# Feed-forward output of a two-layer trunk: one 512-column matmul for the high and low left tiles, two adds for its two halves

## What is computed

```python
D_MODEL, SEQ, DEPTH, D_FF = 1024, 512, 2, 2816

def swiglu(h, w_in, w_out):
    gate, up = jnp.split(h @ w_in, 2, axis=-1)
    return (jax.nn.silu(gate) * up) @ w_out

for layer in range(DEPTH):
    x = x + 0.5 * swiglu(rmsnorm(x, norm_ffn1[layer]), w_ffn1_in[layer], w_ffn1_out[layer])
    x = x + mixer(rmsnorm(x, norm_mix[layer]))          # retention, then sparse attention
    x = x + 0.5 * swiglu(rmsnorm(x, norm_ffn2[layer]), w_ffn2_in[layer], w_ffn2_out[layer])
return rmsnorm(x, final_norm)
```

## Time and profile before

| | |
|---|---|
| median of 3 runs | 1930.58 us |
| lowest, highest | 1929.31, 1930.98 us |
| the profiled execution, its own time | 1932.33 us |
| span of its profile, first to last instruction | 1929.5 us |
| TensorE (PE) busy | 1908.6 us |
| VectorE (DVE) busy | 1590.9 us |
| ScalarE (ACT) busy | 992.3 us |
| GpSimd (POOL) busy | 189.5 us |
| mean granted TensorE clock | 0.998 of 2.4 GHz |

### The profile page before, as it was taken

The page is one execution under the profiler, slowest core; times in us unless marked ns, Lnnn a source line. Parts: engine busy times, 40 slices in busy tenths (PEclk is TensorE's granted clock), DMA queues, the critical chain, the costliest instruction groups (busy, mean ns, idle before and its releaser), DMA issues.

```text
span 1929.5 us, 27001 instructions
## 1 busy us (share of the span) xinstructions
PE 1908.6 (99%) x10772; PEld 1666.0 (86%) x10772; DVE 1590.9 (82%) x1903; ACT 992.3 (51%) x1296; POOL 189.5 (10%) x164
## 2 busy tenths in 40 slices
PE   9999999999999999999999999999999999999998
PEld 7888899888888888888899888889997898888998
...
GB/s 207 207 205 235 214 207 181 118 137 44 137 44 137 95 123 91 205 207 193 254 166 180 177 231 182 207 258 150 177 84 88 1 45 256 202 191 200 264 185 84
DMA packets 100524, 316.63 MB, mean 164 GB/s; under 512 B 5936, under 2 KB 14128, under 8 KB 97328
## 3 DMA queue, kind: packets, MB, share of 16 engines
...
...
## 4 chain that ended last, share of the span: by engine, by line
PE 91%; DVE 4%; ACT 2%; issue 2%; DMA 1%; POOL 1%; SPq 0%; DVEq 0%; POOLq 0%; ACTq 0%
PE bank L2819 14%; PE bank L2821 14%; PE bank L2820 14%; PE bank L2987 7%; PE bank L2989 7%; PE bank L2988 7%; PE bank L2811 4%; PE bank L2813 4%; PE bank L2812 4%; PE bank L3043 3%; PE bank L3045 3%; PE bank L3044 3%; PE bank L2920 2%; PE bank L3054 1%; DVE part_lo L1809 1%
## 5 line engine op out<-in xcount | busy, mean ns | idle before, releaser
L1206 ACT ACTIVATE part_hi<-quad_w 128x1024 fp32r<-128x1024 f32 x280 | 293.1, 1064 | 280.5 <-PE bank L2821 196.4
L1809 DVE TENSOR_TENSOR part_lo<-quad_w,part_hi 128x1024 fp32r<-128x1024 f32 x280 | 329.9, 1217 | 25.5 <-ACT part_hi L1206 25.3
L2819 PE MATMUL bank<-part_hi,s_hi 128*128 128x512 f32 x640 | 252.4, 394 | 0.6 <-DVE part_lo L1809 0.6
L2821 PE MATMUL bank<-part_hi,s_lo 128*128 128x512 f32 x640 | 249.4, 390 | 0.0
L2820 PE MATMUL bank<-part_lo,s_hi 128*128 128x512 f32 x640 | 249.1, 389 | 0.0
L2819 PE MATMUL bank<-part_hi,xn_hi 128*128 128x512 f32 x608 | 238.1, 392 | 2.4 <-DVE part_lo L1809 2.3
L2821 PE MATMUL bank<-part_hi,xn_lo 128*128 128x512 f32 x608 | 237.3, 390 | 0.0
L2820 PE MATMUL bank<-part_lo,xn_hi 128*128 128x512 f32 x608 | 237.1, 390 | 0.0
L1971 DVE TENSOR_TENSOR quad_w<-quad_w,quad_w 128x1024 f32<-128x1024 f32 x160 | 188.5, 1216 | 1.1
L1233 ACT ACTIVATE part_hi<-quad_w 128x1024 fp32r<-128x1024 f32 x84 | 87.0, 1058 | 148.7 <-PE bank L2813 105.9
L2821 PEld LDWEIGHTS bank<-part_hi,s_lo 128*128 128x128 f32 x640 | 120.1, 188 | 25.3
...
...
## 6 DMA issues: line engine op xcount, KB each, us to landing
...
```

The costliest lines, as they stand in the source:

```text
L1206: nc.scalar.activation(in_four(part_hi[part_slot(h)]), source, copy).then_inc(part_hi_made, 1)
L1809: nc.vector.tensor_tensor(in_four(part_lo[part_slot(h)]), source, in_four(part_hi[part_slot(h)]).bitcast(FP32), ALU.subtract)\
L2819: mm(to, hi, in_four(part_hi[slot])[:, :, part], start=start, stop=False, skip_group_check=joins)
L2821: return mm(to, lo, in_four(part_hi[slot])[:, :, part], start=False, stop=stop, skip_group_check=joins)
```

## The change

High and low left tiles are moved by one matmul. Where the weight tile `out_hi` met `left_hi` (L2987) and then the low tile (L2988) in two matmuls of 256 columns into the same 256 sums, it now meets both in one matmul of 512 columns. The moving operand is an access pattern over a common tensor, `left_arena`, with two runs of 256 columns; the two results go into the two halves of a whole bank. The third matmul (`out_lo` with `left_hi`) is added to the lower half as before. The two halves are added only when the bank is read: `add_out` issues two adds, one for each half, the second waiting for the first (`link`).

A tile `dt` now takes a bank of its own. Y has banks 0 to 3, and V and Z share the upper four (`upper_banks`), so that S1T1 must wait for the adds P2 that read x12w21 from the same banks, a wait that was not there before. Some more waits are changed for the same reason: steps of x11w11 and x12w21 wait for the instructions that last read their banks, the last group's turned tiles go to four banks instead of two, and a sublayer behind a feed-forward block waits until the first half of its last add is made. P1 a moves four places back in VectorE's queue. Step 3 of the chain Z in the last block keeps the old form (`one_width`).

```diff
@@ -250,9 +249,7 @@
-    left_hi = [at(f"left_hi{n}", a, HALF_TILES * HALF_SEQ, FP32R)
-               for n, a in enumerate((room, room + 2 * left_size))]
-    left_lo = [at(f"left_lo{n}", a, HALF_TILES * HALF_SEQ, FP32R) for n, a in enumerate(left_lo_at)]
+    left_hi_at = (room, room + 2 * left_size)
...
@@ -265,6 +262,17 @@
+    arena_at = left_lo_at[1]
+    arena_width = (left_hi_at[1] + left_size - arena_at) // 4
+    left_arena = at("left_arena", arena_at, arena_width, FP32R)
+
+    def of_arena(offset, width):
+
+        return left_arena[:, (offset - arena_at) // 4:(offset - arena_at) // 4 + width]
+
+    left_hi = [of_arena(a, HALF_TILES * HALF_SEQ) for a in left_hi_at]
+    left_lo = [of_arena(a, HALF_TILES * HALF_SEQ) for a in left_lo_at]
+    gated_lo = of_arena(gated_at, FF_TILES * SEQ)
...
@@ -374,7 +382,8 @@
     t_sums = nc.dram_tensor("t_sums", (SUBLAYERS.count("ffn") * len(T_SUMS) * OUT_TILES, P, OUT_UNIT), FP32).ap()
-    bank = [ctx.enter_context(nc.psum_tensor(f"bank{n}", [P, SEQ], FP32)) for n in range(8)]
+    banks = ctx.enter_context(nc.psum_tensor("banks", [P, 8 * SEQ], FP32))
+    bank = [banks[:, SEQ * n:SEQ * (n + 1)] for n in range(8)]
     def sem(name):
         return ctx.enter_context(nc.semaphore(name))
@@ -620,13 +629,29 @@
         half, tokens = {"S3T3": (0, 0), "x22T4": (1, 1), "S4w22": (1, 0)}[name]
         return gated_tiles(gated_lo, half, tokens, *LEFT_BATCHES[p][j])
-    def left_low_tile(p, k):
+    def left_low_at(p, k):
         name = OUT_PRODUCTS[p]
         if name in ("x11w11", "x12w21", "S1T1", "S2T2"):
-            return cols(left_lo[p % 2], k, HALF_SEQ)
+            return left_lo_at[p % 2] + 4 * HALF_SEQ * k
         half, tokens = {"S3T3": (0, 0), "x22T4": (1, 1), "S4w22": (1, 0)}[name]
-        return cols(gated_lo, HALF_TILES * half + k)[:, HALF_SEQ * tokens:HALF_SEQ * (tokens + 1)]
+        return gated_at + chunk * (HALF_TILES * half + k) + 4 * HALF_SEQ * tokens
+
+    def left_parts(p, k):
+
+
+        both = sorted([left_hi_at[p % 2] + 4 * HALF_SEQ * k, left_low_at(p, k)])
+        return bass.AP(left_arena, (both[0] - arena_at) // 4,
+                       [[arena_width, P], [(both[1] - both[0]) // 4, 2], [1, HALF_SEQ]])
+
+    def left_low_tile(p, k):
+
+        return bass.AP(left_arena, (left_low_at(p, k) - arena_at) // 4, [[arena_width, P], [1, HALF_SEQ]])
+
+    def one_width(s, chain, dt):
+
+
+        return chain == "Z" and s == len(SUBLAYERS) - 1 and dt == OUT_TILES - 1
     def chain_of(p):
@@ -637,14 +662,17 @@
         return [(0, 2), (2, 3), (3, 4)] if chain == "Z" and s == len(SUBLAYERS) - 1 else [(0, 2), (2, 4)]
+    def upper_banks(s):
+
+        return (4, 5, 6, 7) if s + 1 < len(SUBLAYERS) and SUBLAYERS[s + 1] == "ret" else (6, 7, 4, 5)
+
     def out_bank(s, chain, dt):
-        if chain == "Z" and s == len(SUBLAYERS) - 1 and dt == OUT_TILES - 1:
-            return 6, 0
-        first = {"Y": 0, "V": 2, "Z": 4}[chain]
-        if s + 1 < len(SUBLAYERS) and SUBLAYERS[s + 1] == "ret":
-            first = {"Y": 0, "V": 4, "Z": 2}[chain]
-        return first + dt // 2, dt % 2
+        return dt if chain == "Y" else upper_banks(s)[dt]
+
+    def turned_bank(s, g, half, n):
+
+        return 6 + n if g < GROUPS - 1 else upper_banks(s)[2 * half + n]
     def x_adds(s):
@@ -1322,7 +1350,8 @@
                         to = gated_raw[:, :].rearrange("p (n t) -> p n t", n=FF_TILES)
                         first = GROUP_TILES * g + 2 * n
                         nc.scalar.activation(to[:, first:first + 2, HALF_SEQ * half:HALF_SEQ * (half + 1)],
-                                             bank[6 + n][:, :].rearrange("p (n t) -> p n t", n=2), copy)\
+                                             bank[turned_bank(s, g, half, n)].rearrange("p (n t) -> p n t", n=2),
+                                             copy)\
                             .then_inc(gated_stored, 1)
                 def store_rest():
@@ -2102,14 +2131,17 @@
                     (a, b), chain = piece, chain_of(p)
-                    n, first = out_bank(s, chain, a)
+                    n = out_bank(s, chain, a)
                     columns, tokens = {"x11": (0, 0), "x12": (1, 0), "x21": (0, 1), "x22": (1, 1)}[name]
                     x = x_res[:, :].rearrange("p (k t) -> p k t", k=CHUNKS)
                     to = x[:, OUT_TILES * columns + a:OUT_TILES * columns + b,
                            HALF_SEQ * tokens:HALF_SEQ * (tokens + 1)]
-                    made = bank[n][:, :].rearrange("p (d t) -> p d t", d=2)[:, first:first + b - a]
+                    made = banks[:, SEQ * n:SEQ * (n + b - a)].rearrange("p (d i t) -> p d i t", d=b - a, i=2)
                     dve.wait_ge(unit_done, u0 + OUT_TILES * p + b)
-                    done = nc.vector.scalar_tensor_tensor(to, made, factor, to, ALU.mult, ALU.add)
+                    done = nc.vector.scalar_tensor_tensor(to, made[:, :, 0], factor, to, ALU.mult, ALU.add)
+                    if not one_width(s, chain, a):
+                        link(done)
+                        done = nc.vector.scalar_tensor_tensor(to, made[:, :, 1], factor, to, ALU.mult, ALU.add)
                     if part is None:
                         done.then_inc(x_updated, b - a)
                     else:
@@ -2200,11 +2232,11 @@
                 gated_2(GROUPS - 1)
                 out_low(3)
                 two = pieces(s, "Y")
-                add_out("x11", 0, two[0], "P1", 0.5)
                 out_low(4)
                 out_low(5)
                 left_low(1, 0)
                 left_low(1, 1)
+                add_out("x11", 0, two[0], "P1", 0.5)
                 sum_left("S1")
                 out_low(6)
                 add_out("x11", 0, two[1], "P1", 0.5)
@@ -2857,6 +2889,8 @@
             u0 = FIRST_UNIT[s]
             g0, m = groups_before(s), sums_before(s)
             norm = ("norm", s)
+            if s > 0 and SUBLAYERS[s - 1] == "ffn":
+                pe.wait_ge(x_updated, CHUNKS * (s - 1) + OUT_TILES + 2)
             if kind == "ffn":
                 f = ffn_of(s)
                 parts0 = PARTS * f
@@ -2913,11 +2947,13 @@
                     from_, made = ((v, gated1_made), (p5, gated2_made))[half]
                     pe.wait_ge(made, 2 * (GROUPS * f + g + 1))
+                    if g == GROUPS - 1:
+                        pe.wait_ge(up1_made, 2 * (g0 + GROUPS))
                     for n in range(2):
                         pe.wait_ge(gated_stored, TURNED * f + 4 * g + 2 * half + n + 1)
                         for m in range(2):
                             for t in range(2):
-                                done = nc.tensor.transpose(tile(bank[6 + n], 2 * m + t),
+                                done = nc.tensor.transpose(tile(bank[turned_bank(s, g, half, n)], 2 * m + t),
                                                            tile(from_[t], 2 * n + m), identity[:, :])
                         done.then_inc(gated_turned, 1)
@@ -2955,14 +2991,19 @@
                     p, dt = i // OUT_TILES, i % OUT_TILES
                     name, chain = OUT_PRODUCTS[p], chain_of(p)
-                    n, first = out_bank(s, chain, dt)
                     piece = next(q for q in pieces(s, chain) if q[0] <= dt < q[1])
                     ab = "ab"[dt // 2]
-                    if name == "x11w11":
+                    if name == "x11w11" and dt == 0:
                         pe.wait_ge(gate1_made, 2 * (g0 + GROUPS))
+                    elif name == "x11w11" and dt == 2:
+                        pe.wait_ge(gate2_summed, 2 * (g0 + GROUPS))
                     elif name == "x12w21" and dt == 0:
                         pe.wait_ge(up1_made, 2 * (g0 + GROUPS))
-                        pe.wait_ge(gate2_summed, 2 * (g0 + GROUPS))
+                        pe.wait_ge(gated_stored, TURNED * (f + 1) - 2)
+                    elif name == "x12w21" and dt == 2:
+                        pe.wait_ge(gated_stored, TURNED * (f + 1))
+                    elif name == "S1T1":
+                        pe.wait_ge(x_added, x_added_count(s, f"x11 P2 {ab}"))
                     elif name == "S2T2":
                         pe.wait_ge(x_added, x_added_count(s, f"x11 P1 {ab}"))
                     elif name == "S3T3":
@@ -2972,20 +3013,24 @@
                     elif name == "S4w22":
                         pe.wait_ge(x_added, x_added_count(s, f"x22 P5 {piece[0]}"))
                     pe.wait_ge(w_lo_made, u0 + i + 1)
-                    to = cols(bank[n], first, HALF_SEQ)
-                    opens = name in ("x11w11", "x12w21", "S1T1") and dt == piece[0]
-                    closes = dt == piece[1] - 1
-                    joins = name in ("S2T2", "S3T3", "x22T4", "S4w22")
+                    both = bank[out_bank(s, chain, dt)]
+                    to = cols(both, 0, HALF_SEQ)
+                    opens = name in ("x11w11", "x12w21", "S1T1")
+                    joins = not opens
                     _, hi, lo = out_bufs(i)
```

(12 more changed lines are left out.)

1 line of the change is left out of this document (removed).

## The result

The changed kernel takes 1953.16 us (median of 5 runs, 1951.58 to 1956.14), the kernel before 1930.98 us (5 runs, 1929.31 to 1933.57). The ratio is 1.0117, with a 95% interval of 1.0105 to 1.0129: slower by 22 us, inside the range forecast (1936 to 1956) and 5.3 us above the forecast of 1947.9. The profiled executions differ by 21.9 us of span.

The account below looks back on a forecast made before the run. TensorE, busy for 99% of the span, was taken as the bound. Waits net of TensorE's savings gave +10.9 us and the clock +6.4, so 1930.6 + 17.3 = 1947.9 us, range 1936 to 1956.

Parts of the forecast that it names:

- TensorE's work: Output part, 28 units (0 to 27) per block: 1210 matmul pairs each 0.0133 us shorter, 16.1 us in all at most.
- 0.146 less per unit: Each output unit on TensorE shrinks from 3.96 to 3.816 us.
- units 9 to 15: Output units after unit 8, not held by VectorE: forecast to save 4.0 us over the four blocks.
- VectorE's work: Each output add becomes two linked adds: a pair costs 1.31 us, 0.71 more than one add.
- 40 adds: The forecast's count of VectorE's output adds, said to be on no path by themselves.
- The new wait at unit 8: S1T1 waits for add P2 a to free its bank: 4.56 us later in block 0, 2.50 in others, 12.06 in all.
- Unit 18: It waits for add P6 b, 0.71 us lost per block; with units 16, 17 and 19, +1.7 us in all.
- The block's ends: Last adds delay the next work by 2.13, 1.42 and about 0.5 us in blocks 0, 2 and 3: sum 4.05.
- The clock: TensorE's clock falls after the idle at unit 8, 1.6 us lost per block: 6.4 us, bounds 0 and 12.8.
- It falls more often or longer: Rival, chance 0.12: clock falls more often or longer, at block ends too; +10.9 + 9 to 16 us, 1950 to 1957.
- the case that the forecast gave 0.50: Clock lost at unit 8 as forecast, once per block: +17.3 us, 1947.9 us.
- faster: Rival, chance 0.07: unit 8 doesn't wait in effect, 1914.5 us; decided by a pair costing no more than one add, 1926.1.

Follow-up runs that it names:

- Experiments 8: Against experiment 6's kernel: adds P2 b and x21 b also moved up in VectorE's queue; 1920.55 us, ratio 0.9945 to the kernel before.
- 9: Against experiment 8's kernel: the 512-column matmul written as two of 256 columns; 1931.45 us, ratio 1.0004 to the kernel before.
- experiment 2: Against the kernel before: each add to the stream made twice with half the factor, the second linked behind the first; 1940.07 us, ratio 1.0044.
- experiments 1: Against the changed kernel: the two adds of P2 a moved ahead of the sum S2 in VectorE's queue; 1940.47 us, ratio 1.0051 to the kernel before.
- 6: Against the changed kernel: adds P2 a, P6 a and P6 b moved up in VectorE's queue; 1929.49 us, ratio 0.9994 to the kernel before.
- experiment 10: Against the kernel before: only the add x21 b moved ahead of out_low(26); 1930.08 us, ratio 0.9999.
- Experiment 4: Against the changed kernel: 14 more 512-column matmuls ahead of unit 8's wait for P2 a; 1944.96 us, ratio 1.0086 to the kernel before.
- experiment 3: Against the changed kernel: the second add of each pair left out; 1930.24 us, ratio 0.9996 to the kernel before.

## Why the prediction came out right

**TensorE's work.** Units of 3.82 us came where forecast, but only half the time. Two stretches of block 0 in the changed kernel, the first short, the second long (answers to the earlier trace rows):

```profile
249.18 0.39 PE L3032 MATMUL banks<-left_arena,out_hi_C 128*128 128x512 f32 x1
249.41 0.27 PE L3034 MATMUL banks<-left_arena,out_lo_C 128*128 128x256 f32 x1
249.52 0.39 PE L3032 MATMUL banks<-left_arena,out_hi_C 128*128 128x512 f32 x1
```

```profile
318.72 0.40 PE L3032 MATMUL banks<-left_arena,out_hi_E 128*128 128x512 f32 x1
318.96 0.28 PE L3034 MATMUL banks<-left_arena,out_lo_E 128*128 128x256 f32 x1
319.08 0.40 PE L3032 MATMUL banks<-left_arena,out_hi_E 128*128 128x512 f32 x1
```

0.34 to 0.35 us for the three products of a tile, and 0.35 to 0.36. Of the undisturbed units 4 to 26 of all blocks 38 took 3.81 to 3.82 us and 37 took 3.88 to 3.89. The term "0.146 less per unit" was too large for half of them: units 9 to 15 saved 2.65 us, not 4.0. Experiments 8 and 9 give the term as a whole: 10.9 us of the 16.1. The figure of the Trainium skill that the forecast set against its own price (TensorE: Matmul & The Clock Gate, "Back-to-back issue gap": 2.5 ns on top of the columns for an isolated matmul, an estimate of 3 us in all) is too small for this stream with a weight load for each matmul: the two experiments give 9 ns for each of 1210.

**VectorE's work.** A pair takes 0.71 + 0.61 us (268.61, 269.32, 269.93), as worked out, with the second add starting 0.03 after the end of the first. The pairs on x12 and x21 have 0.79 between their starts, 0.08 more than forecast. The forecast's 40 adds (ten per block in the text ahead of it) are a miscount: the kernel before makes 58, 14 in each block and 16 in the last, and 56 of them are pairs now, which is VectorE's 38.6 us of added busy time (1629.5 for 1590.9). No sum used the 40.

**The new wait at unit 8**: right in mechanism. That the sum came out so close, 11.65 for 12.06, was luck: two errors of opposite sign nearly cancel, -1.8 in block 0 and +1.3 in block 5. Blocks 2 and 3 came at 2.54 and 2.62 for 2.50. Block 0 was overrated (2.73 for 4.56): the profile before had VectorE idle 0.50 us for a load just ahead, and I carried that idle over. In the profile after there is no such idle, and the work there ran 1.8 us earlier (`out_lo_E` at 246.13 for 247.92). In block 5 the same kind of load was late, and VectorE idled 0.98 us for `out_hi_D` at 1830.87 (3.76 for 2.50). Idle for a load isn't a constant of the kernel. That the shared bank makes this wait, and not the adds alone, experiment 2 shows; that it is a matter of place in the queue, experiments 1 and 6. A rival that these leave out is a late load, and block 5 shows its share, some 1 us.

**Unit 18**: +2.0 for +1.7, with the waits of 0.7 to 0.8 us forecast at about 1.

**The block's ends**: unit 20 on came to +3.2 where +1.7 was forecast. Block by block the forecast was +1.7, +1.0, +0.1 and -1.0, measured are +2.1, +0.1, +2.1 and -1.0. In block 3 the clock fell behind the 1.95 us wait for `w_lo` at 1419.83, 1.7 us, at a place where the forecast had no fall; what it had left to the range were the ends of blocks 0 and 2. Block 2 was overrated: TensorE idled 1.33 us there, not some 2.3. So this sum too is closer than its parts. At the end of block 0 the clock stayed up behind 2.7 us, as forecast.

**The clock** was the step with the wrong size: 8.1 us at unit 8 for 6.4 (1.7, 1.5, 2.8 and 2.2), because the low stretch was twice as long in blocks 3 and 5; with the 1.7 us at 1419.83 it makes 9.8 us. The bounds of 0 and 12.8 held it. Its evidence that waits of 1.1 us do nothing doesn't hold everywhere: in experiment 10 the clock fell at the same wait of 1.12 us that had left it up in the kernel before. With 9.8 us of clock the run is in fact the rival "It falls more often or longer" (0.12), whose 1950 to 1957 holds 1953.16, and not the case that the forecast gave 0.50. ("The HAM clock gate" in TensorE: Matmul & The Clock Gate, of the Trainium skill, cited in the forecast, has idling bring half rate; the traces agree with 0.50, though not at every idle, as experiment 1 shows.) Experiment 4 shows cause and size together: with the idle filled, 8.2 us come back and unit 8 is still held by VectorE. The rival "faster" fell with experiment 3, since its condition, a pair at the price of one add, gives 1930.24.

Together: in the traces the sum is 4.5 us above the forecast's 17.3. The clock makes +3.4 of it (9.8 for 6.4), the long units 9 to 15 +1.3, the waits at unit 8 -0.4 and all else +0.2. The medians are 22.2 apart, 0.3 more than the spans.
